# GLA half of the output projection as fourteen quarter products instead of eight tile sums

## The chip, the cores and the metric

One core of one Trainium2 chip runs the whole program in one launch. The metric is the device time of that launch in microseconds (us). The kernel before took 746.36 us (median of three runs, 745.25 to 747.27).

## The reference

One encoder layer on x of 512 tokens by 1024 columns, all in float32. What matters here is the mixer's output projection and what feeds it:

```python
y_na  = neighbourhood_attention(q, k, v, rpb)        # 512 x 512
y_gla = gla_mixer(...)                               # 512 x 512
x = x + concatenate([y_na, y_gla], axis=-1) @ w_out  # w_out is 1024 x 1024
x = x + hierarchical_moe(rmsnorm(x), ...)            # 32 experts, top 2 of one group
return rmsnorm(x, final_norm_g)
```

The GLA half of the projection is y_gla (512 x 512) times the lower 512 rows of w_out (512 x 1024), added onto x. The attention half needs y_na, which is complete only when all eight heads are done.

## The kernel before, in words

Each engine has its own program, run in order; semaphores tie them together. The stages are: input projections and GLA (to about 184 us), neighbourhood attention (184 to 238 us), the attention half of the output projection with router (238 to 281 us), and 32 experts (281 us to the end). The change lies in the attention stage.

Attention runs over 16 units: four pairs of heads (`pair`), each with four blocks of 128 queries (`b`). TensorE's loop over turns i = 2 to 19 (L965 to L999) does in turn i, in this order: on even turns the scores of units i and i+1 (`na_scores`, L914, into banks 2 to 5); one piece of the GLA half (`gla_share`, L948); the four transposes of unit i-2 (L979, bank 6); and the probabilities-times-values product of unit i-3, called PV below (L994). The 64 partitions of a head and the 128 columns of a block make a quarter of the bank that PV writes, so a pair of heads fills one bank. Two banks, 7 and 1 (`Y_BANK`), are used in turn by pairs, and the first PV of pair 2 or 3 waits until ScalarE has emptied the bank of the pair two before (`yn_evicted`, L988).

`gla_share(n)` is half of the sum for one tile of 128 tokens and 512 columns: two matmuls of 128x512. Sixteen such pieces, in turns 3 to 18, give eight tiles, six of them through bank 0, the last two through banks 2 and 3. A matmul of float32 operands stands as two records in the profile, so a piece is four records of line L960.

ScalarE's loop (L1407) does in its turn i, in this order: the copy of the transposed probabilities of unit i-2 out of bank 6 (L1413); the two exponentials of unit i (L1393); and, on turns 7, 11, 15 and 19, the copy of a finished pair out of its Y bank (L1420), which needs PV of unit i-4.

VectorE's loop (L1731) does in its turn i: the addition of a finished GLA tile onto x1 (on eight of the turns, L1742); scale and bias of unit i's scores out of PSUM (L1749, which signals `s_added`); the maximum (L1753); and reciprocal and scaling of the exponentials of unit i-1 (L1727 and a tensor_tensor). All tensor_tensor operations of VectorE's program go through a helper and show the line L1535.

After the loop TensorE does the attention half (`out_proj`, L1001, line L1005 in the profile), and SyncE, once the last PV and the last GLA piece are done (L571, L572), starts the stream of expert weights.

Seven products of quarters are already used for four other projections (`product`, L687, records of line L694): the same order of sums, the same matmuls of 128 by 256 columns.

Of the kernel before, what the change touches and what calls it, by code (L numbers as in the profile page):

```python
# [12 lines left out]
ALU = mybir.AluOpType  # L13
# [58 lines left out]
FIRST_FREED = [(0, 1), (1, 2), (2, 4)]  # L72
IN_HALVES = range(4, 6)
LR_TURN = 3
GLA_BANK = [0] * 6 + [2, 3]
GATE_BANK, HIDDEN_BANK, ROW_BANK = 0, 4, [3, 7]
MIXED = 1
KT_BANK = [6, 7, 4, 5]
RANK_BANK = [2, 2, 0, 1, 2]
Y_BANK = [7, 1]  # L80
SHARE_BANK = [1, 2, 6, 3, 7, 5, 0, 4]


# [14 lines left out]
FIRST_BANK, MIDDLE_BANK, OTHER_BANK = ({QK: 0, GATE: 3, NEAR_Q: 1, NEAR_K: 3}, {QK: 1, GATE: 1, NEAR_Q: 4, NEAR_K: 2},  # L98
                                       {QK: 2, GATE: 0, NEAR_Q: 0, NEAR_K: 1})
TARGET = {1: (0, 0), 2: (0, 0), 6: (0, 1), 3: (0, 1), 7: (1, 1), 5: (1, 1), 4: (1, 0)}  # L100


def products(g, p):
# [86 lines left out]
def mixer_and_moe(nc, x, x_T, rpb, w_in, w_g2, b_g, gla_g, g_mix, w_out, g_ffn_T, w_r, b_r, w_all, g_fin,  # L190
                  c_small, c_mask, c_scan, c_tok, out, limit=SLOTS):
    with ExitStack() as ctx:
# [10 lines left out]
        def at(kib, *shape):  # L203
# [7 lines left out]
            if len(shape) == 3:  # L211
# [36 lines left out]
        token_sum = [None] + [at(144 + 4 * i, HALF_K, HALF_T) for i in range(4)]  # L248
        weight_sum = {g: [None] + [at(kib + 4 * i, HALF_K, HALF_N) for i in range(2)]
                      for g, kib in ((QK, 160), (GATE, 168), (NEAR_Q, 78), (NEAR_K, 126))}  # L250
        gla_gb = at(216, DV)
        s_prev = at(160, 4, NCH, DV)
        yT_near = at(160, TT, KC // 2, P)
# [213 lines left out]
        def target(g, p):  # L467
# [6 lines left out]
            near = na_q if g == NEAR_Q else na_k  # L474
            return near[:, 2 * j:2 * j + 2].rearrange("p m (w r) -> p m w r", r=ROWS)[:, :, :, i * ROWS // 2:(i + 1) * ROWS // 2]

        def product_of(g, p):

            v = pbank[product_bank(g, p)][:]
            if g in (QK, GATE):  # L480
                return v.rearrange("p (m c) -> p m c", m=2)
            return v.rearrange("p (m r w) -> p m w r", m=2, w=GRID_W)
# [14 lines left out]
        def _(sp):  # L497
# [71 lines left out]
            for half in range(2):  # L569
                sp.dma_start(w_on[:, half], wout_d[:, 0:KC // 2, half * 512:(half + 1) * 512]).then_inc(wout_in, 16)  # L570
            sp.wait_ge(pv_done, 4 * PAIRS)  # L571
            sp.wait_ge(og_done, 2 * TT)  # L572
            load_half(1, 0)
            load_half(1, 1)
            load_d(1)
# [110 lines left out]
        def _(pe):  # L686
# [260 lines left out]

            def gla_share(n):  # L948

                j, part = divmod(n, 2)  # L950
                if n == 0:
                    pe.wait_ge(wog_in, 32)
                if part == 0:
                    if GLA_BANK[j]:
                        pe.wait_ge(s_added, 2 * (NU - 1))
                    elif j >= 1:
                        pe.wait_ge(og_added, j)
                t, half = divmod(j, 2)
                for k in (2 * part, 2 * part + 1):
                    mm = pe.matmul(pbank[GLA_BANK[j]][:], yT_gla[:, k, t * P:(t + 1) * P],  # L960
                                   w_og[part][:, k % 2, half * 512:(half + 1) * 512], start=(k == 0), stop=(k == KC // 2 - 1))
                if part == 1:
                    mm.then_inc(og_done, 1)

            for i in range(2, NU + 4):  # L965
                if 4 <= i < NU and i % 2 == 0:
                    na_scores(i)
                    na_scores(i + 1)
                if 3 <= i < NU + 2:
                    gla_share(i - 3)  # L970
                if 0 <= i - 2 < NU:
                    u = i - 2
                    pe.wait_ge(p_scaled, u + 1)
                    if u >= 1:
                        pe.wait_ge(pT_evicted, u)
                    for par in range(2):
                        for c in range(2):
                            a = 2 * par + c
                            mm = pe.transpose(pbank[6][:, a * P:(a + 1) * P],  # L979
                                              probs[u % 4][:, par, c * P:(c + 1) * P], ident)  # L980
                    mm.then_inc(pT_done, 1)
                if 0 <= i - 3 < NU:
                    u = i - 3
                    pair, b = divmod(u, BLOCKS)
                    pe.wait_ge(pT_evicted, u + 1)
                    if u in (1, 2):
                        pe.wait_ge(v_vec, 2 * u + 2)
                    if b == 0 and pair >= 2:  # L988
                        pe.wait_ge(yn_evicted, pair - 1)
                    v0 = KEY_START[b] * ROWS // 64  # L990
                    for c in range(2):
                        for par in range(2):
                            h = 2 * pair + par
                            mm = pe.matmul(pbank[Y_BANK[pair % 2]][64 * par:64 * par + 64, b * P:(b + 1) * P],  # L994
                                           na_v[:, v0 + 2 * c, h * NA_DIM:(h + 1) * NA_DIM], probsT[u % 2][:, 2 * par + c],
                                           start=(c == 0), stop=(c == 1))
                    mm.then_inc(pv_done, 1)
                if i == NU + 2:
                    gla_share(i - 3)  # L999

            def out_proj(t, half, ks=range(KC // 2)):  # L1001
                if t >= 2:
                    pe.wait_ge(x1_done, 2 * (t - 2) + half + 1)
                for k in ks:
                    mm = pe.matmul(pbank[2 * (t % 2) + half][:], yT_near[:, t, k],  # L1005
                                   w_on[:, half, k], start=(k == 0), stop=(k == KC // 2 - 1))
                if ks[-1] == KC // 2 - 1:
                    mm.then_inc(wo_done, 1)
# [29 lines left out]

            pe.wait_ge(yn_evicted, PAIRS)
            pe.wait_ge(wout_in, 32)  # L1040
            pe.wait_ge(og_added, 6)

            for t in range(2):
                if t == 1:
                    pe.wait_ge(og_added, 2 * TT)
                for half in range(2):
                    out_proj(t, half)
            x1_T(0)
# [250 lines left out]
        def _(act):  # L1299
# [107 lines left out]
            for i in range(2, NU + 4):  # L1407
                if i - 2 < NU:
                    u = i - 2
                    act.wait_ge(pT_done, u + 1)  # L1410
                    if u >= 2:
                        act.wait_ge(pv_done, u - 1)
                    nc.scalar.copy(probsT[u % 2].rearrange("p a b -> p (a b)"), pbank[6][:]).then_inc(pT_evicted, 1)  # L1413
                if i < NU:
                    na_exp(i)
                if i >= 4 and (i - 4) % BLOCKS == BLOCKS - 1:
                    pair = (i - 4) // BLOCKS
                    act.wait_ge(pv_done, i - 3)
                    by_column = "p (w t r) -> p w t r"
                    nc.scalar.copy(yT_near[:, :, pair].rearrange("p t (r w) -> p w t r", w=GRID_W),  # L1420
                                   pbank[Y_BANK[pair % 2]][:].rearrange(by_column, t=TT, r=ROWS // TT)).then_inc(yn_evicted, 1)

            def square(t, half):
                act.wait_ge(x1_done, 2 * t + half + 1)
# [108 lines left out]
        def _(dve):  # L1533
# [174 lines left out]
            def v_between(b):  # L1708
# [4 lines left out]
                if b < BLOCKS - 1:  # L1713
                    nc.vector.tensor_copy(na_v[0:64, 2 * b + 1], na_v[64:128, 2 * b]).then_inc(v_vec, 1)

            v_between(0)
            v_between(1)
            NU = PAIRS * BLOCKS
            nc.vector.tensor_copy(upper_b[:], upper).then_inc(router_ready, 1)
            nc.vector.memset(ones_b[:], 1.0).then_inc(router_ready, 1)  # L1720
            dve.wait_ge(g2_in, 32)
# [9 lines left out]
            for i in range(NU + 5):  # L1731
                if i == 2:
                    scale_probs(1)
                    v_between(2)
                if i == 3:
                    v_between(3)
                if i % 2 and i >= 5:
                    j = (i - 5) // 2
                    dve.wait_ge(og_done, j + 1)
                    dve.wait_ge(x_in_sb[j // 2], 32)  # L1740
                    xv = x1[:, j // 2, (j % 2) * 512:(j % 2 + 1) * 512]
                    tt(xv, xv, pbank[GLA_BANK[j]][:], ALU.add).then_inc(og_added, 1)  # L1742
                if i < NU:
                    pair, b = divmod(i, BLOCKS)
                    dve.wait_ge(s_done, i + 1)
                    if i >= 4:
                        dve.wait_ge(pT_done, i - 3)
                    for par in range(2):
                        nc.vector.scalar_tensor_tensor(probs[i % 4][:, par], pbank[2 + 2 * (i % 2) + par][:, 0:NKEY], NA_DIM ** -0.5,  # L1749
                                                       bias[:, 2 * pair + par, BIAS_VAR[b]], ALU.mult,  # L1750
                                                       ALU.add).then_inc(s_added, 1)
                    dve.wait_ge(s_added, 2 * (i + 1))
                    nc.vector.tensor_reduce(nmax[:, i], probs[i % 4], AX.X, ALU.max, negate=True).then_inc(nmax_done, 1)  # L1753
                if 1 <= i <= NU and i != 2:
                    scale_probs(i - 1)
# [75 lines left out]
                then(nc.vector.tensor_copy(rstd_part[2], rstd_rest[1]))  # L1831
                then(nc.vector.tensor_copy(eid, eidx[:, :, 0:2]))

            dve.wait_ge(og_added, 2 * TT)

            def residual(t, half):
                dve.wait_ge(wo_done, 2 * t + half + 1)
                xv = x1[:, t, half * 512:(half + 1) * 512]
                tt(xv, xv, pbank[2 * (t % 2) + half][:], ALU.add).then_inc(x1_done, 1)

            def mean_square(t):
                dve.wait_ge(sumsq_done, TT + 2 * (t + 1))
# [384 lines left out]
```

## Time and profile before

| what | us |
|---|---|
| median of three runs | 746.36 |
| the profiled execution, its own time | 745.2 |
| span of its profile | 742.8 |
| TensorE busy | 728.1 |
| VectorE busy | 237.2 |
| ScalarE busy | 146.9 |
| attention stage, first transposes to last GLA piece (184.81 to 238.22) | 53.4 |

Busy time of TensorE is that of pipelined instructions, whose records overlap by some 0.1 us: the time that a group occupies the engine is read from its start to the start of the next group. The span leaves out 2.4 us that lie around it in the execution's own time.

### The profile page before, as it was taken

The numbers are of one execution on the slowest core, as the hardware profiler recorded it, in microseconds if no ns is written. First come the engines' busy times: TensorE is split into PE (matmuls) and PEld (weight loads), VectorE is DVE, ScalarE is ACT, GpSimd is POOL, SyncE is SP. The second block draws the span as 40 slices with busy tenths as digits, with TensorE's granted clock in tenths as the row PEclk, the third lists the DMA queues.
The fourth block names the chain that finished last, engine by engine and source line by source line (L and its number), as shares of the span: only waits on it lengthen the run. The fifth ranks groups of instructions, "written<-read, shape, count | busy, mean of one in ns | idle before, by whom it ended". The sixth has DMA issues, their size and how long they took to land.

```text
span 742.8 us, 11529 instructions
## 1 busy us (share of the span) xinstructions
PE 728.1 (98%) x5029; PEld 393.8 (53%) x5029; DVE 237.2 (32%) x499; ACT 146.9 (20%) x315; POOL 79.1 (11%) x79
## 2 busy tenths in 40 slices
PE   9999999999999999999999999999999999999995
PEld 4488888854555565455454454454544544544431
DVE  2884464134773466112112012012111111111205
ACT  2652230223553641000000000000000000000014
POOL 0000040910000210100100101001001010010003
PEclk9999999999999999999999999999999999999998
DMA  9833322140901989999999999999999999999995
GB/s 326 259 113 105 143 95 99 72 179 13 408 33 34 429 325 359 410 429 426 415 428 426 440 422 439 430 431 429 430 422 423 436 422 426 426 425 427 423 367 219
DMA packets 31732, 240.78 MB, mean 324 GB/s; under 512 B 5590, under 2 KB 6998, under 8 KB 21184
## 3 DMA queue, kind: packets, MB, share of 16 engines
q1 hardware_dynamic: 29056, 235.94, 77.2%
q0 software_dynamic: 2480, 4.06, 1.4%
q8 instruction: 42, 0.69, 0.4%
q14 instruction: 10, 0.08, 0.0%
q10 hardware_dynamic: 144, 0.00, 0.0%
HBM read 231.74 MB, written 12.32 MB: 329 GB/s over the span
## 4 chain that ended last, share of the span: by engine, by line
PE 88%; DMA 8%; ACT 2%; DVE 1%; SPq 0%; issue 0%; DVEq 0%
PE bank L1161 26%; PE bank L1181 14%; PE bank L694 13%; PE bank L1102 9%; DMA arena<-in_w_all 6%; PE bank L960 4%; PE bank L705 4%; PE bank L1005 4%; PE bank L748 2%; PE bank L1115 2%; DMA arena<-in_x 1%; PE bank L1170 1%; PE bank L994 1%; PE bank L921 1%; PE bank L979 1%; PE bank L1035 1%
## 5 line engine op out<-in xcount | busy, mean ns | idle before, releaser
L1161 PE MATMUL bank<-arena 128*64 128x512 f32 x1024 | 226.7, 593 | 2.2 <-DMA arena<-in_w_all 2.0
L1161 PEld LDWEIGHTS bank<-arena 128*64 128x64 f32 x1024 | 73.3, 137 | 147.1 <-issue 146.8
L1181 PE MATMUL bank<-arena 128*64 128x512 f32 x512 | 116.9, 598 | 0.2
L694 PE MATMUL bank<-arena 128*128 128x256 f32 x448 | 98.6, 380 | 0.0
L694 PEld LDWEIGHTS bank<-arena 128*128 128x128 f32 x448 | 84.5, 190 | 12.6 <-issue 1.3
L1102 PEld LDWEIGHTS bank<-arena 128*128 128x128 bf16 x1344 | 75.3, 98 | 22.2 <-issue 21.9
L1970 DVE SCALAR_TENSOR_TENSOR arena<-bank,arena 128x256 f32<-128x256 f32 x32 | 15.5, 484 | 215.1 <-ACT arena L1489 215.1
L1489 ACT ACTIVATE arena<-bank,arena 128x256 f32<-128x256 f32 x32 | 15.2, 474 | 337.9 <-PE bank L1161 332.0
L1102 PE MATMUL bank<-arena 128*128 128x128 bf16 (+1 forms) x1344 | 81.6, 217 | 0.0
L1535 DVE TENSOR_TENSOR arena<-arena 128x512 f32<-128x512 f32 (+8 forms) x97 | 69.3, 748 | 12.8 <-ACT arena L1302 6.1
L2145 POOL DMA_INDIRECT y_tok<-arena x31 | 30.3, 976 | 402.2 <-DVE arena L1977 387.3
L1181 PEld LDWEIGHTS bank<-arena 128*64 128x64 f32 x512 | 33.9, 136 | 58.5 <-issue 54.8
L1977 DVE COPY arena<-bank 128x512 f32<-128x512 f32 x32 | 22.1, 692 | 117.7 <-PE bank L1181 117.7
L1535 DVE TENSOR_TENSOR arena<-bank,arena 128x512 f32<-128x512 f32 (+1 forms) x46 | 30.5, 665 | 70.0 <-PE bank L694 27.3
L960 PE MATMUL bank<-arena 128*128 128x512 f32 x64 | 31.6, 617 | 0.0
L1005 PE MATMUL bank<-arena 128*128 128x512 f32 x64 | 28.6, 595 | 0.0
L748 PE MATMUL bank<-arena 128*128 128x512 f32 x64 | 28.0, 593 | 0.5 <-DMA arena<-in_w_in 0.5
L705 PE MATMUL bank<-arena 128*128 128x512 f32 x64 | 27.9, 594 | 0.0
L1494 ACT COPY arena<-bank 128x256 f32<-128x256 f32 x32 | 11.9, 373 | 62.2 <-PE bank L1170 62.2
L1302 ACT ACTIVATE arena<-bank 128x512 f32<-128x512 f32 x16 | 9.5, 596 | 70.8 <-PE bank L694 70.8
L2131 POOL TENSOR_TENSOR arena<-arena 128x256 f32<-128x256 f32 x24 | 21.4, 927 | 17.8 <-DVE arena L1535 17.8
L2138 POOL TENSOR_TENSOR arena<-arena 128x512 bf16<-128x512 f32 x8 | 9.3, 1158 | 118.3 <-ACT arena L1445 118.3
(182 smaller groups left out, 503.3 us busy)
## 6 DMA issues: line engine op xcount, KB each, us to landing
arena<-in_w_all SPq DMA_DIRECT2D x47, 2048.0 KB, 28.9
arena<-in_w_all SPq DMA_DIRECT2D x7, 6144.0 KB, 26.0
arena<-in_w_all SPq DMA_DIRECT2D x8, 4096.0 KB, 27.6
arena<-in_w_all SPq DMA_DIRECT2D x19, 1024.0 KB, 9.9
arena<-in_w_in SPq DMA_DIRECT2D x5, 2048.0 KB, 8.4
arena<-in_w_all SPq DMA_DIRECT2D x9, 512.0 KB, 7.7
arena<-in_x SPq DMA_DIRECT2D x8, 512.0 KB, 6.4
arena<-in_w_out SPq DMA_DIRECT2D x4, 1024.0 KB, 15.0
```

The costliest lines, as they stand in the source:

```text
L694: mm = pe.matmul(pbank[product_bank(g, p)][:, tile * 256:(tile + 1) * 256], lhs, rhs, start=(p in (1, 2, 5) and tile == 0 and k == 0), sto ...
L705: mm = pe.matmul(pbank[b % UNIT_BANKS][:], hT_cols[:, k, b * P:(b + 1) * P], w[:, k], start=(k == 0), stop=(k == KC - 1))
L748: mm = pe.matmul(pbank[2 + t][:], gx[:, k, t * P:(t + 1) * P], w_buf[0][:, k], start=(k == 0), stop=(k == KC - 1))
L960: mm = pe.matmul(pbank[GLA_BANK[j]][:], yT_gla[:, k, t * P:(t + 1) * P], w_og[part][:, k % 2, half * 512:(half + 1) * 512], start=(k == 0) ...
L1005: mm = pe.matmul(pbank[2 * (t % 2) + half][:], yT_near[:, t, k], w_on[:, half, k], start=(k == 0), stop=(k == KC // 2 - 1))
L1102: mm = pe.matmul(pbank[ROW_BANK[half]][:, k * P:k * P + n], h2_part[t][i][:, KC // 2 * half + k], pick[:, t, 0:n], start=(t == 0 and k == ...
L1161: mm = pe.matmul(both, xT[:, k, rows], gate_and_up(e, k)[:, :, cols], start=(k == 0), stop=(k == KC - 1))
L1181: mm = pe.matmul(pbank[down_bank(e)][64 * half:64 * half + 64, :], hidT[:, kc % 2, kc // 2], down_unit(e)[:, kc, half * 512:(half + 1) * 512],
L1535: return nc.vector.tensor_tensor(out_, a, b, op)
L1977: nc.vector.tensor_copy(y_sb[e % RING], pbank[down_bank(e)][:]).then_inc(y_evicted, 1)
L2131: nc.gpsimd.tensor_tensor(bias[:, h, v].rearrange("p (j r) -> p j r", r=ROWS), run, mask[:, v].rearrange("p (j r) -> p j r", r=ROWS), ALU. ...
L2145: nc.gpsimd.indirect_dma_start(y_tok, bass.IndirectOffsetOnAxis(ap=tab_u[:, e:e + 1], axis=0), y_sb[e % RING], None, bounds_check=last_row ...
```

## The change

The GLA half is split for each half of 512 columns (h = 0, 1) into quarters: 256 tokens or columns by 256 of the inner dimension. Seven products per half replace the eight quarter products, fourteen in all. Each product is four matmuls of 128x256 (eight records) in the turns of `SHARE_TURNS`, and each is added onto its quarter of x1 by VectorE. Products 1, 6, 7 and 4 of a half accumulate in one bank, so that each addition brings in the running sum; 2, 5 and 3 do so in the other. The two halves swap banks 0 and 1. VectorE gets six differences of weights and four sums of y_gla to form, and one more difference of weights per half. With bank 1 taken, all pairs of heads share bank 7 for PV.

```diff
-GLA_BANK = [0] * 6 + [2, 3]
-RANK_BANK = [2, 2, 0, 1, 2]
-Y_BANK = [7, 1]
+RANK_BANK = [0, 0, 2, 1, 2]
+Y_BANK = 7
+SHARE_ORDER = [(h, p) for h in range(2) for p in (1, 2, 6, 5, 7, 3, 4)]
+SHARE_TURNS = [3, 4, 5, 6, 7, 9, 10, 11, 12, 14, 15, 16, 17, 18]
+def share_bank(h, p):
+    return h if p in (1, 6, 7, 4) else 1 - h
...
-            sp.wait_ge(og_done, 2 * TT)
+            sp.wait_ge(og_done, len(SHARE_ORDER))
...
             def gla_share(n):
-                j, part = divmod(n, 2)
+                h, p = SHARE_ORDER[n]
                 if n == 0:
                     pe.wait_ge(wog_in, 32)
...
+                if n >= 2:
+                    pe.wait_ge(og_added, n - 1)
+                if p in (3, 4, 5, 6, 7):
+                    pe.wait_ge(sums_done, max(sums("Y", {5: 1, 6: 2, 7: 3}.get(p, 4)), sums(f"share{h}", 4 if p == 4 else 2)))
+                a, w = share_tokens(p), share_weights(h, p)
+                for tile in range(2):
+                    for k in range(2):
+                        mm = pe.matmul(pbank[share_bank(h, p)][:, tile * 256:(tile + 1) * 256], a[:, k, tile * P:(tile + 1) * P],
+                                       w[:, k], start=(p in (1, 2, 5) and tile == 0 and k == 0), stop=(tile == 1 and k == 1),
+                                       skip_group_check=p in (6, 7, 4, 3))
+                mm.then_inc(og_done, 1)
...
-                if 3 <= i < NU + 2:
-                    gla_share(i - 3)
+                if i in SHARE_TURNS[:-1]:
+                    gla_share(SHARE_TURNS.index(i))
...
-                    if b == 0 and pair >= 2:
-                        pe.wait_ge(yn_evicted, pair - 1)
+                    if b == 0 and pair >= 1:
+                        pe.wait_ge(yn_evicted, pair)
...
             def out_proj(t, half, ks=range(KC // 2)):
-                    mm = pe.matmul(pbank[2 * (t % 2) + half][:], yT_near[:, t, k],
+                    mm = pe.matmul(pbank[2 * ((t + 1) % 2) + half][:], yT_near[:, t, k],
...
-            pe.wait_ge(og_added, 6)
...
+            def share_weight_sums(h):
+                tt(share_sum[h][1], share_quarter(h, 0, 1), share_quarter(h, 0, 0), ALU.subtract).then_inc(sums_done, 1)
+                tt(share_quarter(h, 0, 1), share_quarter(h, 1, 1), share_quarter(h, 0, 1), ALU.subtract).then_inc(sums_done, 1)
+                dve.wait_ge(sums_done, sums(f"share{h}", 1))
+                tt(share_sum[h][2], share_quarter(h, 1, 1), share_sum[h][1], ALU.subtract).then_inc(sums_done, 1)
+            def y_sums():
+                low, high = slice(0, 2), slice(2, 4)
+                dve.wait_ge(yg_evicted, GLA_HEADS)
+                tt(y_sum[1], yT_gla[:, low, late], yT_gla[:, high, late], ALU.add).then_inc(sums_done, 1)
+                tt(y_sum[3], yT_gla[:, low, early], yT_gla[:, low, late], ALU.subtract).then_inc(sums_done, 1)
+                dve.wait_ge(sums_done, sums("Y", 1))
+                tt(y_sum[2], y_sum[1], yT_gla[:, low, early], ALU.subtract).then_inc(sums_done, 1)
+                dve.wait_ge(sums_done, sums("Y", 2))
+                tt(y_sum[4], yT_gla[:, high, early], y_sum[2], ALU.subtract).then_inc(sums_done, 1)
+            def add_share(n):
...
+                dve.wait_ge(og_done, n + 1)
+                tt(share_target(h, p), share_target(h, p), pbank[share_bank(h, p)][:].rearrange("p (t c) -> p t c", t=2),
+                   ALU.add).then_inc(og_added, 1)
+                if p == 2:
+                    tt(share_quarter(h, 1, 0), share_quarter(h, 1, 0), share_sum[h][2], ALU.subtract).then_inc(sums_done, 1)
+            dve.wait_ge(wog_in, 32)
+            dve.wait_ge(y_done, 16)
+            share_weight_sums(0)
+            share_weight_sums(1)
             v_between(0)
             v_between(1)
...
                 if i == 3:
+                    y_sums()
                     v_between(3)
-                if i % 2 and i >= 5:
...
+                if i - 1 in SHARE_TURNS:
+                    add_share(SHARE_TURNS.index(i - 1))
```

## Rows read from the trace of the kernel before

**Rows 1.** The page: busy time and the chain that ended last, by engine

```profile
PE 728.1 (98%) x5029; PEld 393.8 (53%) x5029; DVE 237.2 (32%) x499; ACT 146.9 (20%) x315; POOL 79.1 (11%) x79
PE 88%; DMA 8%; ACT 2%; DVE 1%; SPq 0%; issue 0%; DVEq 0%
```

**Rows 2.** Windows: start:end, length, each engine's busy us (instructions), clock, DMA share, GB/s

```profile
184.80:238.20 53.40, 53.31 (x306) 29.70 (x305) 35.74 (x78) 27.10 (x76) 0.00 (x0) 1.00 0.40 158
738.00:742.80 4.80, 0.00 (x0) 0.00 (x0) 0.94 (x2) 0.27 (x1) 0.00 (x0) 0.57 0.58 224
```

**Rows 3.** Timeline of TensorE: start us, duration, operation, count; turns 6 and 7

```profile
194.49 0.66 PE L994 MATMUL bank<-arena 128*64 128x128 f32 x8
195.08 1.13 PE L921 MATMUL bank<-arena 64*128 64x256 f32 x8
196.14 1.98 PE L960 MATMUL bank<-arena 128*128 128x512 f32 x4
197.96 0.60 PE L979 MATMUL bank<-arena 128*128 128x128 f32 x4
198.49 0.66 PE L994 MATMUL bank<-arena 128*64 128x128 f32 x8
199.08 1.98 PE L960 MATMUL bank<-arena 128*128 128x512 f32 x4
200.90 0.60 PE L979 MATMUL bank<-arena 128*128 128x128 f32 x4
201.43 0.66 PE L994 MATMUL bank<-arena 128*64 128x128 f32 x8
202.02 1.13 PE L921 MATMUL bank<-arena 64*128 64x256 f32 x8
```

**Rows 4.** Timeline of TensorE: turn 4's scores, products of quarters, attention half

```profile
188.13 1.13 PE L921 MATMUL bank<-arena 64*128 64x256 f32 x8
82.98 7.07 PE L694 MATMUL bank<-arena 128*128 128x256 f32 x32
89.98 1.22 PE L806 MATMUL bank<-arena 64*64 64x64 f32 x68
238.22 13.90 PE L1005 MATMUL bank<-arena 128*128 128x512 f32 x32
251.96 1.04 PE L1016 MATMUL bank<-arena 128*128 128x128 f32 x8
```

**Rows 5.** Groups of TensorE's weight loads, line L694: count, busy us, mean ns

```profile
L694 PEld LDWEIGHTS bank<-arena 128*128 128x128 f32 x358 | 67.4, 190 | 9.8 <-issue 0.9
```

**Rows 6.** Timeline of ScalarE: its turn 7

```profile
201.54 0.59 ACT L1413 COPY arena<-bank 128x512 f32<-128x512 f32 x1 [1.36 <-PE bank L979]
202.02 0.51 ACT L1393 ACTIVATE arena<-arena 128x256 f32<-128x256 f32 x1
202.92 0.19 ACT L1393 ACTIVATION_READ_ACCUMULATOR arena<-arena 128x1 f32 x1
203.01 1.03 ACT L1420 COPY arena<-bank 128x512 f32<-128x512 f32 x1
```

**Rows 7.** Chain that ended last, in order of time: start, us, what

```profile
235.18 0.59 ACT arena L1413
235.81 0.66 PE bank L994 x8
```

**Rows 8.** Timeline of VectorE: turns 3 to 5

```profile
186.00 0.42 DVE L1712 COPY arena<-arena 64x512 f32<-64x512 f32 x1
186.45 0.75 DVE L1749 SCALAR_TENSOR_TENSOR arena<-bank,arena 128x256 f32<-128x256 f32 x2
188.88 0.76 DVE L1749 SCALAR_TENSOR_TENSOR arena<-bank,arena 128x256 f32<-128x256 f32 x2 [0.16 <-PE bank L921]
189.67 0.69 DVE L1753 TENSOR_REDUCE arena<-arena 128x2 f32<-128x512 f32 x1
190.28 0.15 DVE L1727 RECIPROCAL arena<-arena 128x2 f32<-128x2 f32 x1
190.47 0.69 DVE L1535 TENSOR_TENSOR arena<-arena 128x512 f32<-128x512 f32 x1
191.22 0.69 DVE L1535 TENSOR_TENSOR arena<-arena,bank 128x512 f32<-128x512 f32 x1
191.82 0.42 DVE L1749 SCALAR_TENSOR_TENSOR arena<-bank,arena 128x256 f32<-128x256 f32 x1
```

**Rows 9.** Timeline of VectorE: before the attention stage

```profile
160.99 0.42 DVE L1714 COPY arena<-arena 64x512 f32<-64x512 f32 x1
167.25 0.42 DVE L1712 COPY arena<-arena 64x512 f32<-64x512 f32 x1 [5.84 <-ACT arena L1388]
```

**Rows 10.** Waits of TensorE over the span, longest: total us, times, longest one

```profile
PE bank L1161 <- DMA arena<-in_w_all: 2.0, 3, 1.2
```

More of the change, by code:

```diff
@@ L100 @@
 TARGET = {1: (0, 0), 2: (0, 0), 6: (0, 1), 3: (0, 1), 7: (1, 1), 5: (1, 1), 4: (1, 0)}
+SHARE_ORDER = [(h, p) for h in range(2) for p in (1, 2, 6, 5, 7, 3, 4)]
+SHARE_TURNS = [3, 4, 5, 6, 7, 9, 10, 11, 12, 14, 15, 16, 17, 18]
+SUMS += [("share0", 1), ("share0", 3), ("share0", 2), ("share1", 1), ("share1", 3), ("share1", 2),
+         ("Y", 1), ("Y", 3), ("Y", 2), ("Y", 4), ("share0", 4), ("share1", 4)]
+def share_bank(h, p):
+    return h if p in (1, 6, 7, 4) else 1 - h
 def products(g, p):
@@ L250, in mixer_and_moe @@
                       for g, kib in ((QK, 160), (GATE, 168), (NEAR_Q, 78), (NEAR_K, 126))}
+        y_sum = [None] + [at(kib, 2, HALF_T) for kib in (128, 130, 132, 197)]
+        share_sum = [[None] + [at(187 + 4 * h + 2 * i, 2, HALF_N) for i in range(2)] for h in range(2)]
         gla_gb = at(216, DV)
@@ L475, in target, with share_tokens, share_quarter, share_weights @@
             return near[:, 2 * j:2 * j + 2].rearrange("p m (w r) -> p m w r", r=ROWS)[:, :, :, i * ROWS // 2:(i + 1) * ROWS // 2]
+        def share_tokens(p):
+            if p in (1, 2, 4):
+                return yT_gla[:, 0 if p == 1 else 2:2 if p == 1 else 4, HALF_T if p == 4 else 0:T if p == 4 else HALF_T]
+            return y_sum[{5: 1, 6: 2, 7: 3, 3: 4}[p]]
+        def share_quarter(h, i, j):
+            return w_og[i][:, :, h * 512 + j * HALF_N:h * 512 + (j + 1) * HALF_N]
+        def share_weights(h, p):
+            if p in (5, 6):
+                return share_sum[h][p - 4]
+            return share_quarter(h, *{1: (0, 0), 2: (1, 0), 3: (1, 1), 4: (1, 0), 7: (0, 1)}[p])
+        def share_target(h, p):
+            i, j = TARGET[p]
+            return x1[:, 2 * i:2 * i + 2, h * 512 + j * HALF_N:h * 512 + (j + 1) * HALF_N]
         def product_of(g, p):
@@ L948, in gla_share @@
             def gla_share(n):
-                j, part = divmod(n, 2)
+                h, p = SHARE_ORDER[n]
                 if n == 0:
                     pe.wait_ge(wog_in, 32)
[L953 to L963, printed above, removed]
+                if n >= 2:
[9 more added lines that the diff above has]
+                mm.then_inc(og_done, 1)
             for i in range(2, NU + 4):
@@ L993, in _ @@
                             h = 2 * pair + par
-                            mm = pe.matmul(pbank[Y_BANK[pair % 2]][64 * par:64 * par + 64, b * P:(b + 1) * P],
+                            mm = pe.matmul(pbank[Y_BANK][64 * par:64 * par + 64, b * P:(b + 1) * P],
                                            na_v[:, v0 + 2 * c, h * NA_DIM:(h + 1) * NA_DIM], probsT[u % 2][:, 2 * par + c],
@@ L997, in _ @@
                     mm.then_inc(pv_done, 1)
-                if i == NU + 2:
-                    gla_share(i - 3)
+                if i == SHARE_TURNS[-1]:
+                    gla_share(len(SHARE_ORDER) - 1)
             def out_proj(t, half, ks=range(KC // 2)):
@@ L1040, in _ @@
             pe.wait_ge(wout_in, 32)
-            pe.wait_ge(og_added, 6)
             for t in range(2):
                 if t == 1:
-                    pe.wait_ge(og_added, 2 * TT)
+                    pe.wait_ge(og_added, len(SHARE_ORDER))
                 for half in range(2):
@@ L1420, in _ @@
                     nc.scalar.copy(yT_near[:, :, pair].rearrange("p t (r w) -> p w t r", w=GRID_W),
-                                   pbank[Y_BANK[pair % 2]][:].rearrange(by_column, t=TT, r=ROWS // TT)).then_inc(yn_evicted, 1)
+                                   pbank[Y_BANK][:].rearrange(by_column, t=TT, r=ROWS // TT)).then_inc(yn_evicted, 1)
             def square(t, half):
@@ L1714, in v_between @@
                     nc.vector.tensor_copy(na_v[0:64, 2 * b + 1], na_v[64:128, 2 * b]).then_inc(v_vec, 1)
+            NU = PAIRS * BLOCKS
+            def share_weight_sums(h):
[13 more added lines that the diff above has]
+            def add_share(n):
+                h, p = SHARE_ORDER[n]
+                if n == 0:
+                    for t in range(TT):
+                        dve.wait_ge(x_in_sb[t], 32)
+                dve.wait_ge(og_done, n + 1)
+                if n:
+                    dve.wait_ge(og_added, n)
+                tt(share_target(h, p), share_target(h, p), pbank[share_bank(h, p)][:].rearrange("p (t c) -> p t c", t=2),
+                   ALU.add).then_inc(og_added, 1)
+                if p == 2:
+                    dve.wait_ge(sums_done, sums(f"share{h}", 2))
+                    tt(share_quarter(h, 1, 0), share_quarter(h, 1, 0), share_sum[h][2], ALU.subtract).then_inc(sums_done, 1)
[3 more added lines that the diff above has]
+            share_weight_sums(1)
             v_between(0)
             v_between(1)
-            NU = PAIRS * BLOCKS
             nc.vector.tensor_copy(upper_b[:], upper).then_inc(router_ready, 1)
@@ L1735, in _ @@
                 if i == 3:
+                    y_sums()
                     v_between(3)
-                if i % 2 and i >= 5:
[L1738 to L1742, printed above, removed]
+                if i - 1 in SHARE_TURNS:
+                    add_share(SHARE_TURNS.index(i - 1))
                 if i < NU:
@@ L1832, in split_rstd @@
                 then(nc.vector.tensor_copy(eid, eidx[:, :, 0:2]))
-            dve.wait_ge(og_added, 2 * TT)
+            dve.wait_ge(og_added, len(SHARE_ORDER))
             def residual(t, half):
@@ L1838, in residual @@
                 xv = x1[:, t, half * 512:(half + 1) * 512]
-                tt(xv, xv, pbank[2 * (t % 2) + half][:], ALU.add).then_inc(x1_done, 1)
+                tt(xv, xv, pbank[2 * ((t + 1) % 2) + half][:], ALU.add).then_inc(x1_done, 1)
             def mean_square(t):
```

## The prediction

> **What bounds the kernel now.** I read the page first: TensorE is busy for 728.1 of 742.8 us and carries 88% of the chain that ended last [rows 1]. Then the window of the attention stage: TensorE busy 53.31 of 53.40 us at a granted clock of 1.00 (the 2.4 GHz level), VectorE 35.74, ScalarE 27.10 [rows 2]. So this stage is TensorE's, and there are two ways to change its length: give it less to do, or make it wait. Then the timeline of TensorE for two turns of the loop, which shows what each piece occupies, from start to next start [rows 3]: GLA piece 199.08 to 200.90, 1.82 us; transposes 200.90 to 201.43, 0.53; PV 201.43 to 202.02, 0.59; scores of two units 195.08 to 196.14, 1.06, so 0.53 each. Two turns take 202.02 - 195.08 = 6.94 us, which is 2 x (1.82 + 0.53 + 0.59) + 1.06. Last the timelines of ScalarE and VectorE, for when the things come that TensorE will wait for.
>
> **TensorE's work.** Sixteen pieces become fourteen. A 128x512 record costs (251.96 - 238.22) / 32 = 0.429 us, a 128x256 record (89.98 - 82.98) / 32 = 0.219 with the group's transition in it [rows 4]. Half of 0.429 is 0.215, so the narrow matmul is nearly as efficient. A piece now is four records, 1.72 us, plus 0.10 of transition; a new one is eight records, 8 x 0.215 + 0.10 = 1.82 us. Gain: 2 x 1.82 = **3.64 us**. Bounds per piece: 1.74 (no transition beyond 8 x 0.2175) and 1.95 (eight records at the 0.219 above and a double transition), which makes 14 pieces 24.4 to 27.3 us against 29.1, a gain of 4.8 to 1.8. I take 3.64, since L694 is the same instruction.
>
> The new pieces load weights twice as often: 112 loads instead of 64. Each takes 190 ns [rows 5], and yet the records of L694 follow each other at 219 ns [rows 4], so the loads run beside the matmuls. The Trainium skill, page "TensorE: Matmul & The Clock Gate", section "Part 3: Packing small matmuls", says that a weight load overlaps a running matmul only if it goes to other rows of the array; these all use the full array. By its section "LDWEIGHTS (loading the stationary operand)", a load of 128 columns takes about 107 ns, and 48 exposed loads would then be an estimate of 5.1 us more, turning the gain into a loss of 1.5. The spacing in rows 4 is against that.
>
> **The new wait for the Y bank.** This is the largest term. Bank 1 is taken, so the first PV of pairs 1, 2 and 3 (TensorE's turns 7, 11 and 15) waits until ScalarE has copied the pair before out of bank 7. That copy is the last thing of ScalarE's turn of the same number, behind the copy of the transposed probabilities and two exponentials. In turn 7 of the trace the transposes end at 201.43; ScalarE takes them from 201.54, does exponentials from 202.02, starts the pair's copy at 203.01 and ends it at 204.04 [rows 6]. PV, which now starts at 201.43 [rows 3], can start there only after 204.04 plus the step from ScalarE to TensorE, 0.04 (235.18 + 0.59 to 235.81 [rows 7]). That is 204.08 - 201.43 = 2.65 us, and 0.07 for the restart (PV 0.66 behind a wait [rows 7], 0.59 otherwise): 2.72. Behind the waiting PV in TensorE's order stand scores, GLA piece and transposes, all of it needed work, and nothing passes it. Three times: **+8.16 us**. Bounds: 2.2 if the pair's copy costs no more than a plain one (0.59 instead of 1.03 [rows 6]), 3.2 if the exponentials in front of it come half a microsecond late; so 6.6 to 9.6. I take the row's own sequence.
>
> **VectorE's new work.** Its operations on 512 elements are 0.60 apart (191.22 to 191.82 [rows 8]). (a) Six differences of weights before the stage, 3.6 us: VectorE idles there 5.84 us, from 161.4 to 167.25 [rows 9], and TensorE is not due for anything of it. Nothing. (b) Four sums of y in its turn 3, 4 x 0.60 + 0.1 for two waits on its own result = 2.5 us. They stand ahead of the scaling of unit 3's scores, which now ends at 186.45 + 0.75 = 187.20 [rows 8]. TensorE needs it to overwrite the bank with unit 5's scores at 188.13 + 0.53 = 188.66 [rows 4]: slack 1.46, less 0.04 for the step. So TensorE waits 2.5 - 1.42 = **1.08 us**, once. Bounds 0.6 to 1.6 (2.0 to 3.0 us for the four). (c) Six more additions and a weight difference in each half. Per two turns VectorE now has 2 x (0.79 + 0.61 + 0.19 + 0.60) = 4.38 us for two units plus 0.60 for one addition [rows 8]; it becomes 5.6, once per half 6.2, against 6.94 of TensorE. It fits. In the two turns that have no GLA piece (8 and 13) TensorE needs 5.12 per two turns against VectorE's 5.0; that is close, but each comes just after a Y wait of 2.7 us in which VectorE catches up. I laid the three engines' orders beside each other with these durations; besides the four waits named it gives one more of **0.15 us**, in turn 13: transposes follow transposes with only PV between, and bank 6 isn't empty yet (0.53 past, then 0.11 + 0.49 + 0.14 until it is, less 0.59). The same layout for the kernel before ends the stage at 238.36; the trace has 238.22.
>
> **What is moved otherwise.** The exchanged banks of the output projection and of the ranks keep the same order of writer and reader: nothing. The removed wait for six additions cost nothing before. The last addition must be done before the third `out_proj`, 3.4 us after the last piece, and takes 0.8: nothing. SyncE starts the expert weights when the last PV and last piece are done; that moves with TensorE's end of stage, so the stream, on which the experts wait 2.0 us in all [rows 10], and TensorE are shifted alike, and the stage's gain or loss reaches the end whole.
>
> **Sum.** -3.64 + 8.16 + 1.08 + 0.15 = +5.75 us. On the profiled execution's own 745.2 (span 742.8 plus 2.4 around it): 750.95. That execution stands 1.2 under the median of the runs; on the median 746.36 I get **752.1 us**.
>
> **Rivals.**
> 1. *The Y bank costs nothing* (not slower). It decides if the pair's copy is done before the transposes of turns 7, 11, 15. PV of the pair's last unit ends at 199.08 [rows 3], and ScalarE sits idle for 1.36 us before 201.54 [rows 6], so there would be room for 1.03. Against it: ScalarE runs in order, and the copy is written behind the exponentials. Then -3.64 + 1.08 + 0.15 = -2.4: 744.0.
> 2. *VectorE becomes the bound.* For it: 35.74 us busy now, plus six additions, four sums and two differences, 7.2 us, makes 42.9, and the shortened pairs of turns have 0.1 us of margin. It decides if its operations on three-dimensional slices take 0.75 instead of 0.60; then every pair of turns is some 0.5 longer, seven of them: +3.5, 755.6. Against it: the Y waits give it slack at the right places.
> 3. *Weight loads are exposed*: 48 x 0.19 [rows 5] = 9.1 more, 761. Against it the spacing in rows 4. The Trainium skill's rule above is this one.
> 4. *The clock falls in the 2.7 us gaps.* After TensorE's last matmul the granted clock fell to a mean of 0.57 in the last 4.8 us [rows 2], so idleness lowers it at some point. If it fell in each gap to the 1.2 GHz level, a turn of some 3.5 us of work behind it would double: 3 x 3.5 = 10.5, 762.6. No wait of TensorE as long as 2.7 us within its work is in the trace, so only that end speaks for it.
> 5. *The narrow matmuls save nothing* (the change doesn't do what it says): 1.95 a piece and a wait for VectorE at each start, 14 x 0.13 + 1.8: 755.7.
>
> **How the numbers follow.** Forecast 0.78; rival 1 0.07; 2 0.07; 3 0.02; 4 0.03; 5 0.03. With each term at its bound the forecast spans -4.8 + 6.6 + 0.6 = +2.4 to -1.8 + 9.6 + 1.6 + 0.2 = +9.6; the terms will not all lean one way, so for 8 in 10 I take +3.0 to +8.6: 749.4 to 755.0. About 0.3% (2.2 us) is what a measurement of this kernel can tell from no change. Rival 1 at 744.0 lies on that edge (744.1) and is shared between faster and same: faster 0.05, same 0.05, slower 0.90.
>
> **What would show it.** In the changed kernel's timeline of TensorE: eight records of the pieces take 1.82 us to the next start; three idle gaps of some 2.7 us ahead of the PV line, released by ScalarE's copy of a pair; one of some 1.1 us ahead of the second scores of turn 4, released by VectorE; two turns at 6.94 elsewhere; granted clock 1.00. The attention half starts at about 244.0 instead of 238.22. I am wrong if the PV gaps are missing, if VectorE releases more than one long wait, or if TensorE meets fewer waits on the expert weights than 2.0 us and so takes part of the loss back.

## The result and the profile after

The changed kernel took 756.04 us (median of five runs, 753.9 to 756.66) against 746.36 us; ratio 1.0127, interval 1.0107 to 1.0147. That is 9.7 us slower. I had forecast 752.1 us and 749.4 to 755.0: the right direction, 3.9 us too little, and outside the range. The profiled execution took 753.9 us with a span of 752.1, so 9.3 us more span than before. Of all executions here and below one, of the kernel before with a single Y bank, fell in a slow state (960.43 us at a mean granted clock of 0.749) and is left out.

The attention stage in one window, columns as in [rows 2]: length, then busy us of TensorE's matmuls and weight loads, VectorE, ScalarE, GpSimd, then the granted clock (the share of TensorE's full clock that it was given, as a mean over the window), DMA share and GB/s.

```profile
184.50:247.40 62.90, 53.70 (x354) 40.94 (x353) 42.37 (x90) 27.21 (x76) 0.00 (x0) 0.95 0.34 134
```

TensorE's busy time has hardly moved (53.31 before), although there is less to do; 9.2 us of the stage are idle, where there was 0.1; and the granted clock, 1.00 before, is 0.95: at a lower clock the same matmuls are busy for longer. From start to start the stage takes 247.40 - 184.52 = 62.88 us against 53.41, which is +9.47, and nothing else in the span changes by more than 0.3. The waits of TensorE in this stage, where the kernel before has none:

```profile
PE bank L1024 <- ACT arena L1449: 8.0, 3, 2.7
PE bank L951 <- DVE arena L1813: 0.9, 1, 0.9
PE bank L1009 <- ACT arena L1442: 0.2, 1, 0.2
```

L1024 is PV, L951 the scores, L1009 the transposes, L990 the pieces. The first and longest wait is the one for the Y bank, in the timeline of TensorE in turns 6 to 9 (start, duration, count), to be held against [rows 3]:

```profile
198.93 0.60 PE L1009 MATMUL bank<-arena 128*128 128x128 f32 x4
199.46 0.66 PE L1024 MATMUL bank<-arena 128*64 128x128 f32 x8
200.05 1.99 PE L990 MATMUL bank<-arena 128*128 128x256 f32 x8
201.88 0.60 PE L1009 MATMUL bank<-arena 128*128 128x128 f32 x4
205.14 0.66 PE L1024 MATMUL bank<-arena 128*64 128x128 f32 x8 [2.66 <-ACT arena L1449]
205.73 1.19 PE L951 MATMUL bank<-arena 64*128 64x256 f32 x8
206.85 1.11 PE L1009 MATMUL bank<-arena 128*128 128x128 f32 x4
207.90 1.12 PE L1024 MATMUL bank<-arena 128*64 128x128 f32 x8
208.95 2.54 PE L990 MATMUL bank<-arena 128*128 128x256 f32 x8
211.32 0.60 PE L1009 MATMUL bank<-arena 128*128 128x128 f32 x4
```

Read from start to start: the piece takes 201.88 - 200.05 = 1.83 us. The gap ahead of PV is 2.66 us and ends 0.15 us after ScalarE's copy of the pair (203.99 + 1.00 = 204.99, PV at 205.14), which stands behind the exponentials as in [rows 6]:

```profile
203.90 0.19 ACT L1422 ACTIVATION_READ_ACCUMULATOR arena<-arena 128x1 f32 x1
203.99 1.00 ACT L1449 COPY arena<-bank 128x512 f32<-128x512 f32 x1
```

Then, in TensorE's rows, comes what I had not expected in such a stage: with no wait at all, the transposes take 1.05 us instead of 0.53, PV 1.05 instead of 0.59, the piece 2.37 instead of 1.83. Everything is slower at once, and the windows of that slow stretch and of the one behind the third gap say why: the granted clock is at half there, the 1.2 GHz level. A row that reads between 0.50 and 1.00 holds time at both levels.

```profile
202.40:205.10 2.70, 0.08 (x1) 0.00 (x0) 0.90 (x2) 2.48 (x6) 0.00 (x0) 1.00 1.06 392
205.70:206.90 1.20, 1.20 (x11) 0.74 (x9) 0.42 (x2) 0.00 (x0) 0.00 (x0) 0.91 0.06 24
206.90:211.30 4.40, 4.40 (x22) 3.38 (x21) 3.90 (x10) 1.57 (x5) 0.00 (x0) 0.64 0.00 0
221.50:226.00 4.50, 4.46 (x36) 3.49 (x36) 2.98 (x7) 0.34 (x1) 0.00 (x0) 1.00 0.00 0
238.00:240.70 2.70, 2.70 (x7) 1.94 (x7) 0.00 (x0) 0.00 (x0) 0.00 (x0) 0.50 0.03 6
240.70:244.00 3.30, 3.30 (x24) 2.69 (x23) 0.78 (x2) 0.59 (x1) 0.00 (x0) 0.98 0.00 0
```

The clock was still 1.00 in the first gap (first row). It fell over a microsecond after TensorE had started again at 205.14: the scores from 205.73 took 1.12 us, nearly their usual 1.06, and the transposes from 206.85 double their usual time (second and third row). Behind the second gap it did not fall (fourth row). From start to start, the stretch behind the first gap costs 0.06 + 0.52 + 0.46 + 0.54 = 1.58 us, that behind the third 1.69.

The whole account of the stage, predicted and read:

| term | predicted | read in the profile |
|---|---|---|
| pieces: 14 against 16, at 1.82 each by the prediction, 14 x 1.83 against 16 x 1.82 read | -3.64 | -3.50 |
| three waits for the Y bank, from start to start | +8.16 | +8.21 |
| wait ahead of unit 5's scores, from start to start | +1.08 | +1.22 |
| turn 13, from start to start | +0.15 | +0.27 |
| granted clock | 0 | +3.27 |
| sum | +5.75 | +9.47 |

From start to start a wait comes out longer than the idle time that the profile prints for it. A group's record normally runs on past the start of the next group (transposes 0.60 us long, next start after 0.53), and ahead of a gap that end is part of the wait: 2.66 + 0.07 = 2.73 us per Y wait.

### The profile page after: what moved, and what is told of

The parts are those of the page before. It is cut to its first block, busy times and chain, and to the rows that moved or that the text cites. A ratio compares the mean times of both kernels' runs of the same rounds, so it can differ in the third digit from the quotient of the medians.

```text
span 752.1 us, 11662 instructions
## 1 busy us (share of the span) xinstructions
PE 728.8 (97%) x5077; PEld 405.3 (54%) x5077; DVE 246.7 (33%) x517; ACT 146.8 (20%) x315; POOL 79.2 (11%) x79
## 4 chain that ended last, share of the span: by engine, by line
PE 85%; DMA 9%; ACT 2%; DVE 2%; issue 1%; SPq 0%; DVEq 0%; POOLq 0%
PE bank L1190 25%; PE bank L1210 13%; PE bank L724 13%; PE bank L1131 9%; DMA arena<-in_w_all 6%; PE bank L778 4%; PE bank L735 4%; PE bank L1035 4%; PE bank L990 4%; PE bank L1144 2%; PE bank L1199 1%; PE bank L1024 1%; PE bank L951 1%; DMA arena<-y_tok 1%; DMA y_tok<-arena 1%; PE bank L1009 1%
## 5 line engine op out<-in xcount | busy, mean ns | idle before, releaser
L724 PE MATMUL bank<-arena 128*128 128x256 f32 x448 | 98.6, 380 | 0.0
L724 PEld LDWEIGHTS bank<-arena 128*128 128x128 f32 x448 | 84.5, 190 | 12.6 <-issue 1.3
L1564 DVE TENSOR_TENSOR arena<-arena 128x512 f32<-128x512 f32 (+8 forms) x109 | 76.2, 735 | 13.1 <-ACT arena L1331 6.1
L990 PE MATMUL bank<-arena 128*128 128x256 f32 x112 | 30.0, 414 | 0.0
L778 PE MATMUL bank<-arena 128*128 128x512 f32 x64 | 28.2, 596 | 0.5 <-DVE arena L1571 0.5
L1035 PE MATMUL bank<-arena 128*128 128x512 f32 x64 | 28.6, 595 | 0.0
L735 PE MATMUL bank<-arena 128*128 128x512 f32 x64 | 27.9, 594 | 0.0
L990 PEld LDWEIGHTS bank<-arena 128*128 128x128 f32 x112 | 21.5, 202 | 5.9 <-issue 2.7
L1564 DVE TENSOR_TENSOR arena<-arena,bank 128x512 f32<-128x512 f32 (+1 forms) x25 | 16.5, 664 | 21.9 <-PE bank L1035 11.4
```

What stands on the lines that cost most here:

```text
L724: mm = pe.matmul(pbank[product_bank(g, p)][:, tile * 256:(tile + 1) * 256], lhs, rhs, start=(p in (1, 2, 5) and tile == 0 and k == 0), sto ...
L735: mm = pe.matmul(pbank[b % UNIT_BANKS][:], hT_cols[:, k, b * P:(b + 1) * P], w[:, k], start=(k == 0), stop=(k == KC - 1))
L778: mm = pe.matmul(pbank[2 + t][:], gx[:, k, t * P:(t + 1) * P], w_buf[0][:, k], start=(k == 0), stop=(k == KC - 1))
L990: mm = pe.matmul(pbank[share_bank(h, p)][:, tile * 256:(tile + 1) * 256], a[:, k, tile * P:(tile + 1) * P], w[:, k], start=(p in (1, 2, 5) ...
L1035: mm = pe.matmul(pbank[2 * ((t + 1) % 2) + half][:], yT_near[:, t, k], w_on[:, half, k], start=(k == 0), stop=(k == KC // 2 - 1))
L1564: return nc.vector.tensor_tensor(out_, a, b, op)
```

## The experiments

Each kernel ran beside the kernel before on the same chip; ratios are to that.

**One part alone: the single Y bank in the kernel before.** The wide pieces, banks and sums stay as they were.

```diff
-Y_BANK = [7, 1]
+Y_BANK = [7, 7]
-                    if b == 0 and pair >= 2:
-                        pe.wait_ge(yn_evicted, pair - 1)
+                    if b == 0 and pair >= 1:
+                        pe.wait_ge(yn_evicted, pair)
```

> The kernel before with one edit: every pair of heads uses bank 7, and the first PV of pairs 1 to 3 waits for the copy of the pair before, as in the changed kernel. The wide GLA pieces stay. Theory (the wait for the Y bank costs its length, 2.7 us three times, and the clock falls behind some of the gaps, 1.6 us each time): 8.2 plus 1.6 to 4.8, so 756.2 to 759.4, with three gaps of 2.7 us released by ScalarE's copy. Rival (the loss lies in the narrow pieces and VectorE's new work, the wait only shows where TensorE would have been late anyway): under 750.

Measured: 756.19 us (median of five executions, 754.96 to 760.60), at the lower edge of what was expected; ratio 1.0156 (1.0127 to 1.0185), with the same three gaps. Without a single narrow matmul it is as slow as the whole change. In its profile the clock falls behind the third gap alone, but for longer:

```profile
PE bank L994 <- ACT arena L1420: 8.0, 3, 2.7
237.54 1.12 PE L994 MATMUL bank<-arena 128*64 128x128 f32 x8 [2.68 <-ACT arena L1420]
238.59 3.78 PE L960 MATMUL bank<-arena 128*128 128x512 f32 x4
242.16 1.06 PE L979 MATMUL bank<-arena 128*128 128x128 f32 x4
243.16 1.00 PE L994 MATMUL bank<-arena 128*64 128x128 f32 x8
244.09 1.99 PE L960 MATMUL bank<-arena 128*128 128x512 f32 x4
237.50:238.60 1.10, 1.06 (x9) 0.76 (x9) 0.00 (x0) 0.00 (x0) 0.00 (x0) 0.50 0.00 0
237.50:243.80 6.30, 6.26 (x22) 3.46 (x24) 0.69 (x1) 0.54 (x1) 0.00 (x0) 0.50 0.00 0
```

PV 1.05, piece 3.57, transposes 1.00, PV 0.93: 3.0 us over their normal times, at a granted clock of 0.50 (last two rows). Its stage takes 64.64 us; 53.41 + 8.2 + 3.0 = 64.6. The rival that the wait only shows where TensorE would have been late anyway is out.

**The wait taken away: the copy of the pair first.** ScalarE's instructions are the same, in another order.

```diff
             for i in range(2, NU + 4):
+                if i >= 4 and (i - 4) % BLOCKS == BLOCKS - 1:
+                    pair = (i - 4) // BLOCKS
+                    act.wait_ge(pv_done, i - 3)
...
                 if i - 2 < NU:
                     u = i - 2
                     act.wait_ge(pT_done, u + 1)
...
-                if i >= 4 and (i - 4) % BLOCKS == BLOCKS - 1:
-                    pair = (i - 4) // BLOCKS
-                    act.wait_ge(pv_done, i - 3)
...
```

> The changed kernel with one edit: in ScalarE's turns 7, 11, 15 and 19 the copy of the finished pair stands ahead of the copy of the transposed probabilities and the exponentials, so that it runs beside TensorE's GLA piece. Theory: the three gaps of 2.7 us go and the slow stretches behind them with them; left are -3.5 for two pieces fewer, +0.9 for the four sums, +0.2 in turn 13: 744.0, granted clock 1.00 in the whole stage. Rival (the narrow pieces and VectorE's additions are the loss): still above 748. Rival of the layout (the exponentials, now one copy later, are late for VectorE and the transposes): new waits of up to 1.0 us three times, 747.

Measured: 742.73 us, ratio 0.9972 (0.9956 to 0.9987): faster than the kernel before, which stood at 745.13 beside it. The stage takes 51.46 us (184.67 to 236.13) against 53.41. ScalarE in its turn 7, to be held against [rows 6]:

```profile
201.19 1.04 ACT L1441 COPY arena<-bank 128x512 f32<-128x512 f32 x1
202.66 0.59 ACT L1448 COPY arena<-bank 128x512 f32<-128x512 f32 x1 [0.43 <-PE bank L1009]
203.14 0.51 ACT L1422 ACTIVATE arena<-arena 128x256 f32<-128x256 f32 x1
```

The copy of the pair now lies in the idle time in which ScalarE waited for transposes; even so 0.43 us of that idle time are left, so nothing behind it is late. The three gaps are gone, two small waits remain, and the clock is 1.00 throughout:

```profile
PE bank L951 <- DVE arena L1813: 0.9, 1, 0.9
PE bank L1009 <- ACT arena L1448: 0.2, 1, 0.2
184.70:236.10 51.40, 50.19 (x354) 38.70 (x353) 42.21 (x90) 27.33 (x76) 0.00 (x0) 1.00 0.40 162
```

**The clock apart from the wait: the gaps filled.** The waits end when they did; TensorE only has something to do in them. The product is written to a free part of a bank and read by nothing.

```diff
                     if b == 0 and pair >= 1:
+                        pe.wait_ge(s_added, 2 * i)
+                        for _ in range(5):
+                            pe.matmul(pbank[2][:, NKEY:2 * NKEY], ident, na_k[:, 0, 0:NKEY], start=True, stop=True)
                         pe.wait_ge(yn_evicted, pair)
```

> The changed kernel with one addition: ahead of each of the three waits for the Y bank TensorE does five matmuls of 128x256 (about 2.2 us) into a free part of a scores bank; nothing reads them. The waits end at the same time as before. Theory (the clock falls because TensorE is idle for 2.7 us): granted clock 1.00 in the stage, the two slow stretches of 1.6 us go, 756.0 - 3.3 = 752.7. Rival (the clock falls in this stage for another reason, the denser weight loads of the narrow pieces or the alternation of short groups): slow stretches stay, 755 to 757.

Measured: 751.17 us, ratio 1.0073 (1.0056 to 1.0091). Fifteen extra matmuls make the kernel 4.9 us faster than the changed one (756.04; the kernel before stood at 745.13 here and at 746.36 there, so some 3.6 beside it).

```profile
202.55 2.32 PE L1021 MATMUL bank<-arena 128*128 128x256 f32 x10
205.28 0.66 PE L1027 MATMUL bank<-arena 128*64 128x128 f32 x8 [0.41 <-ACT arena L1452]
205.87 1.13 PE L951 MATMUL bank<-arena 64*128 64x256 f32 x8
206.94 0.66 PE L1009 MATMUL bank<-arena 128*128 128x128 f32 x4
184.75:244.17 59.42, 56.95 (x384) 44.11 (x383) 42.26 (x90) 27.25 (x76) 0.00 (x0) 1.00 0.36 142
```

PV starts as late as before, the clock stays at 1.00, and the stage takes 59.42 us: the sum of my terms without the clock is 53.41 + 5.75 = 59.16, and that of the terms as read 53.41 + 6.20 = 59.61. Only one execution has a profile, but all six took 750.24 to 751.81 us at a mean granted clock of 0.996 to 0.998, and all five of the changed kernel 753.90 to 756.66 at 0.990 to 0.993. So the 3.3 us are due to TensorE's idleness and not to the narrow matmuls or their weight loads.

**Fewer of them.** The same with two extra matmuls in place of five.

> As fill_gaps, but with two extra matmuls (0.9 us) instead of five ahead of each wait: the gaps shrink from 2.66 to about 1.8 us, PV starts as late as before. Theory (a shorter gap lowers the clock seldom or never): 751 to 752.7, as with five. Rival (any gap above the 0.4 us left in fill_gaps does it): slow stretches as in the changed kernel, 755 to 756.

Measured: 750.97 us, ratio 1.0081 (1.0063 to 1.0098). Gaps of 1.70 us are left and the clock stays up behind all three in its profile. Five of its six executions took 750.72 to 751.26 us; the sixth took 753.75 at a mean clock of 0.994, where the others have 0.997 or 0.998. It has no rows. Three of the 34 executions of the kernel before in these comparisons, which has no gap, also show 0.994 (747.53 to 748.05 us), so it stays open whether a gap of 1.70 us lowered the clock there.

```profile
PE bank L1027 <- ACT arena L1452: 5.1, 3, 1.7
```

**The changed kernel profiled twice more.** No edit.

> The changed kernel once more, unedited, for a second profile: the three gaps of 2.7 us are at the same places to within 0.1 us. Theory (whether the clock falls behind a gap differs from execution to execution): the slow stretches stand behind other gaps, or another number of them, than the first and third; each costs 1.5 to 3 us, and the time moves with them. Rival (the place decides it, by what TensorE did around the gap): again the first and third gap, 1.6 us each.

> As after_look2, a third profile of the changed kernel: its slow stretches again compared by place and length. A time above 755 should have more or longer ones than the 3.3 us of the first profile.

Measured: 753.89 and 752.62 us. The waits for the Y bank are 8.0 us in both. In the second profile the slow stretches stand again behind the first and third gap (first two rows, 1.58 and 1.64 us in all); in the third profile there is one, behind the second gap, which had been clean twice (the other rows):

```profile
205.80 1.58 PE L951 MATMUL bank<-arena 64*128 64x256 f32 x8
237.49 3.45 PE L990 MATMUL bank<-arena 128*128 128x256 f32 x8
220.60 0.66 PE L1024 MATMUL bank<-arena 128*64 128x128 f32 x8 [2.66 <-ACT arena L1449]
221.18 1.25 PE L951 MATMUL bank<-arena 64*128 64x256 f32 x8
222.37 3.52 PE L990 MATMUL bank<-arena 128*128 128x256 f32 x8
225.72 0.60 PE L1009 MATMUL bank<-arena 128*128 128x128 f32 x4
```

The stages take 62.82 and 61.30 us; the second, with one stretch (0.13 + 1.52 us), is 1.5 shorter, and so is the span, by 1.3. The place does not decide it: a gap of this length lowers the clock in some executions and not in others, here behind 5 of 9 gaps.

**Real work in the gap: the piece between transposes and PV.** In turns 7, 11 and 15 only.

```diff
-                if i in SHARE_TURNS[:-1]:
+                if i in SHARE_TURNS[:-1] and i not in (7, 11, 15):
                     gla_share(SHARE_TURNS.index(i))
...
+                if i in (7, 11, 15):
+                    gla_share(SHARE_TURNS.index(i))
                 if 0 <= i - 3 < NU:
```

> The changed kernel with TensorE's order edited in turns 7, 11 and 15: the GLA piece stands between transposes and PV instead of ahead of the transposes, so that its 1.83 us run while PV's bank is being emptied. Theory: each gap shrinks from 2.66 to 0.8 us (5.5 us less in all) and the clock stays at 1.00 (3.3 us less): 756.0 - 8.8 = 747.2. Rival (the clock falls for any wait in this stage): 750 to 751, slow stretches present. Rival (ScalarE's copy comes later because something of it waits for the moved piece): gaps over 1.5 us, 749 or more.

Measured: 747.09 us, ratio 1.0023 (1.0013 to 1.0032). The clock stays up behind all three, as expected, but the gaps are larger than I had worked out:

```profile
PE bank L1026 <- ACT arena L1451: 3.4, 3, 1.4
PE bank L951 <- DVE arena L1815: 0.9, 1, 0.9
PE bank L1009 <- ACT arena L1444: 0.7, 4, 0.2
```

3.4 us in place of 2.5, and three more short waits of 0.2 where transposes now follow PV and transposes with no piece between. The moved piece no longer stands between PV and the transposes behind it, where it had covered the emptying of bank 6; and the transposes now come so early that ScalarE's exponentials ahead of the copy wait for VectorE's maximum, in turn 7 for 0.31 us:

```profile
202.26 0.51 ACT L1424 ACTIVATE arena<-arena 128x256 f32<-128x256 f32 x1 [0.31 <-DVE arena L1819]
```
The stage takes 55.64 us where 54.1 was worked out. That the median still met the expected 747.2 is partly luck: the kernel before stood at 745.36, 1.0 lower than in the first comparison.

**Both waits taken away.** The copy first, and the four sums in VectorE's turn 2.

```diff
                 if i == 2:
                     scale_probs(1)
                     v_between(2)
+                    y_sums()
                 if i == 3:
-                    y_sums()
                     v_between(3)
```

> The changed kernel with the copy of the pair first and, as a second edit, the four sums of y_gla moved from VectorE's turn 3 to its turn 2, where it idles for 6 us while TensorE does the last columns of v. Theory: the wait of 0.9 us ahead of unit 5's scores goes as well: 743.1. Rival (another wait takes its place, VectorE being just in time throughout): 744.0, as without the second edit.

Measured: 741.84 us, ratio 0.9949 (0.9931 to 0.9968), the fastest of all. The sums now run in VectorE's idle time, which still has 3.36 us left, and the stage takes 50.25 us:

```profile
178.71 2.62 DVE L1564 TENSOR_TENSOR arena<-arena 128x512 f32<-128x512 f32 x4
184.69 0.76 DVE L1813 SCALAR_TENSOR_TENSOR arena<-bank,arena 128x256 f32<-128x256 f32 x2 [3.36 <-PE bank L951]
185.00:235.30 50.30, 50.03 (x355) 38.87 (x354) 40.09 (x86) 27.10 (x76) 0.00 (x0) 1.00 0.42 167
```

## Why the prediction was wrong

- **The step that failed** is rival 4, *the clock falls in the 2.7 us gaps*, to which I gave 0.03, and with it the zero that the sum had for the clock. I argued that no wait of that length stands within TensorE's work in the trace, and took the missing row for evidence against the rival. It was evidence of nothing. The only row on the matter [rows 2] said that idleness lowers the clock at some point. The mechanism was worked out too large (10.5 us): the clock fell behind two gaps of three in the first profile, and cost 1.6 us each time, not 3.5. As the fifth row of the table it measures 3.27 us, and filling the gaps gives it back.
- **The Y bank** was right in place, releaser and size, 8.21 us in all for 8.16; that it came so close is partly luck. The prediction's 0.07 for a restart isn't there: it set the length of PV's record (0.66) against a distance of starts (0.59), and PV behind the gap also takes 0.59 from start to start (205.14 to 205.73). The step from ScalarE to TensorE, on the other hand, is 0.15 us and not the 0.04 of [rows 7]. The two nearly cancel. Taken alone it makes the kernel before as slow as the changed one; taken away it makes the changed kernel faster than before. Rival 1 (it costs nothing) is out as a forecast, but its own argument, that ScalarE has idle time for the copy, became the cure.
- **The pieces** were right: 1.83 us each, gain 3.50 of 3.64, so rival 5 (they save nothing) is out. Rival 3 (exposed weight loads, with the Trainium skill's rule on loads overlapping only in other rows of the array, page "TensorE: Matmul & The Clock Gate", section "Part 3: Packing small matmuls") would have made a piece longer by 48 x 0.19 / 14 = 0.65 us; the trace does not agree with it.
- **VectorE's work** was right: the differences of weights are hidden, the four sums cost a wait of 0.94 us, 1.22 from start to start, for 1.08, and rival 2 did not come: with both waits cured TensorE is busy for 50.03 of 50.30 us.
- **Turn 13** costs 0.27 instead of 0.15: 0.18 of idle time, and 0.09 more from start to start, 0.07 of which is the end of PV's record ahead of the wait (0.66 against 0.59).
- **From stage to end.** The stage's 9.47 us reach the span as 9.3; the waits on the expert weights stay at 2.0 us, as said. The profiled execution's own time grew by 8.7, since 1.8 us lie around its span where 2.4 did. The median of the changed kernel lies 2.1 us above its profiled execution, that of the kernel before 1.2. What the remaining 0.9 consists of stays open; the unprofiled executions have no rows.
- **The range** was made of bounds on the terms I had. Its upper end needed the clock term, for which the trace before had no price. Even with every one of those terms at its bound it would have reached +9.6, and +9.7 was measured.

## What to carry to other kernels

A change that takes a buffer away from a dense TensorE stage is priced by the order of the engine that gives the buffer back: read everything that stands ahead of the releasing instruction in its queue, and first ask whether it can simply go first. Here that one move is worth 12 us (ratios 1.0127 and 0.9972), over three times the 3.5 that the algebra saves. And a gap of 2.7 us in TensorE's work can cost more than its length: allow for matmuls at half speed behind it, with a chance of about one in two per gap (6 of 12 here), unless rows of that kernel show the opposite. From what length on this holds isn't shown; the gaps of 1.70 us had none in one profile.

## What the runs showed of the hardware that I had not expected

After gaps of 2.66 us the granted clock fell to 0.50 behind 5 of 9 gaps of the changed kernel and 1 of 3 of the kernel before with one bank, and cost 1.6 to 3.0 us each time; in the profiles, one of each kernel, with three gaps of 1.70 us, with gaps of 1.42, 1.02 and 1.02 us, and with three of 0.4 us it did not fall. It may fall over a microsecond after TensorE has resumed (behind the first gap of the first profile) or be down when it resumes (PV at 1.05 us at once, in the kernel before with one bank). The weight loads of the narrow pieces, 112 for 112 records of 128x256 and 190 ns each by the median, stay hidden: the first piece of the changed kernel goes from 185.01 to 186.74, 0.216 us a record.
